# One-core two-block model: memory attention and index projection in one loop, the set-up in another order, pooled rows fetched apart

## What is computed

```python
# block 1
h = rmsnorm(x, g_mix);  proj = h @ w_in          # split into q_s k_s v_s | q_d k_d v_d | q_i k_i w_i | q_m | gates
o_swa = sliding_window_attention(rope(q_s), rope(k_s), v_s, sinks)      # 8 heads, window 128, blocks of 128
o_dsa = dsa_attention(rope(q_d), rope(k_d), v_d, rope(q_i), rope(k_i), w_i)   # 4 index heads, top 256 keys
o_mem = memory_cross_attention(q_m, mem_k, mem_v)                       # 4 heads, 256 memory rows
x = x + (sum of gate_b * (o_b @ w_proj_b)) @ w_out
x = x + square(relu(rmsnorm(x) @ w_mlp_in)) @ w_mlp_out                 # feed-forward 0
# block 2 (adaLN): mLSTM in two directions and a pooled branch y_b, then
x = x + gt1 * (concat(y_a, y_b) @ w_out_2)
x = x + gt2 * (square(relu(modulate(rmsnorm(x)) @ w_ff1)) @ w_ff2)      # feed-forward 1
```

## Time and profile before

| | us |
|---|---|
| three runs, median (lowest, highest) | 2640.07 (2639.22, 2640.80) |
| profiled execution | 2647.66 |
| its span | 2645.9 |
| PE busy in the span | 2482.5 (94%) |
| DVE, ACT, POOL busy | 1588.8, 1203.2, 834.6 |

### The profile page before, as it was taken

One profiled execution on the slowest core, in us unless ns is written; L12 is line 12 of the kernel. 1 busy time (PEld: TensorE's weight loads), 2 busy tenths in 40 slices (PEclk: granted clock), 3 DMA queues, 4 the chain that ended last, 5 costly groups with the idle time before them and its releaser, 6 DMA issues. The chain is left out here.

```text
span 2645.9 us, 32798 instructions
## 1 busy us (share of the span) xinstructions
PE 2482.5 (94%) x11852; PEld 2023.9 (76%) x11852; DVE 1588.8 (60%) x2820; ACT 1203.2 (45%) x2222; POOL 834.6 (32%) x748
## 2 busy tenths in 40 slices
PE   4997899999899999999999999999898999999997
PEld 3765688887677778887888887778776888878886
DVE  5347458988555687765545776334758444356666
ACT  6136346745511455554333453225526555443343
POOL 0222332221220066663252400005303565514242
PEclk9999899999999999999999999999999999999998
DMA  4102122323263256657754455424242444396354
GB/s 160 47 13 83 35 62 91 97 96 113 97 200 104 80 180 214 198 195 267 255 178 143 153 175 182 77 72 135 73 175 100 157 150 152 133 344 191 132 163 150
DMA packets 191187, 371.91 MB, mean 141 GB/s; under 512 B 13724, under 2 KB 58404, under 8 KB 190772
## 3 DMA queue, kind: packets, MB, share of 16 engines
q1 hardware_dynamic: 178676, 342.56, 39.2%
q10 hardware_dynamic: 8064, 14.68, 1.5%
q0 software_dynamic: 4288, 12.60, 1.5%
HBM read 269.05 MB, written 100.74 MB: 140 GB/s over the span
## 5 line engine op out<-in xcount | busy, mean ns | idle before, releaser
L2797 PE MATMUL bank<-hq_hi,wq_hi 128*128 128x512 f32 x896 | 352.7, 394 | 18.2 <-DVE hq_lo L1938 8.6
L2824 PE MATMUL bank<-ring_b_hi,ring_a_hi 128*128 128x512 f32 x896 | 350.7, 391 | 6.3 <-DVE hidden L1982 5.2
L2798 PE MATMUL bank<-hq_lo,wq_hi 128*128 128x512 f32 x896 | 350.6, 391 | 0.0
L2799 PE MATMUL bank<-hq_hi,wq_lo 128*128 128x512 f32 x896 | 350.5, 391 | 0.0
L2826 PE MATMUL bank<-ring_b_hi,ring_a_lo 128*128 128x512 f32 x896 | 350.1, 391 | 0.0
L2825 PE MATMUL bank<-ring_b_lo,ring_a_hi 128*128 128x512 f32 x896 | 350.1, 391 | 0.0
L2141 DVE TENSOR_TENSOR ring_a_lo<-a_raw,ring_a_hi 128x1024 fp32r<-128x1024 f32 x112 | 153.1, 1367 | 227.5 <-ACT ring_a_hi L1337 227.3
L1337 ACT ACTIVATE ring_a_hi<-a_raw 128x1024 fp32r<-128x1024 f32 x112 | 118.7, 1060 | 336.3 <-PE bank L2826 331.0
L1927 DVE TENSOR_TENSOR wq_lo<-unit_raw,wq_hi 128x512 fp32r<-128x512 f32 x160 | 164.4, 1030 | 108.9 <-ACT wq_hi L1185 106.0
L2797 PEld LDWEIGHTS bank<-hq_hi,wq_hi 128*128 128x128 f32 x896 | 169.4, 189 | 56.6 <-DVE hq_lo L1938 14.6
L2824 PEld LDWEIGHTS bank<-ring_b_hi,ring_a_hi 128*128 128x128 f32 x896 | 169.2, 189 | 42.7 <-DVE hidden L1982 6.1
(11 more groups left out here) (466 smaller groups left out, 5532.9 us busy)
## 6 DMA issues: line engine op xcount, KB each, us to landing
a_raw<-hidden_scratch SPq DMA_DIRECT2D x112, 512.0 KB, 3.3
hidden_scratch<-hidden SPq DMA_DIRECT2D x32, 1024.0 KB, 4.8
w_raw<-in_w_in SPq DMA_DIRECT2D x104, 256.0 KB, 2.8
hidden_scratch<-hidden SPq DMA_DIRECT2D x32, 768.0 KB, 3.6
unit_raw<-in_w_mlp_in SPq DMA_DIRECT2D x16, 1024.0 KB, 5.7
b_raw<-in_w_mlp_out SPq DMA_DIRECT2D x32, 512.0 KB, 4.4
unit_raw<-in_w_ff SPq DMA_DIRECT2D x16, 1024.0 KB, 5.4
b_raw<-in_w_ff SPq DMA_DIRECT2D x32, 512.0 KB, 4.7
```

Source lines behind the costliest of these rows:

```text
L2797: mm(o, lh[:, q, :], rh[:, q, :], start=(fresh and q == 0), stop=False, skip_group_check=True)
L2798: mm(o, lh[:, q, :], rl[:, q, :], start=False, stop=False, skip_group_check=True)
L2799: l = mm(o, ll[:, q, :], rh[:, q, :], start=False, stop=(q == 3), skip_group_check=True)
L2824: mm(o, ra_hi[r][:, e, js], rb_hi[r][:, e, :], start=(fresh and v == 0 and e == 0), stop=False, skip_group_check=True)
```

## The change

It has three parts.

1. **Memory attention and index projection in one loop.** The index weights are split inside the window attention: in each odd round u, ACT does `split_hi` of piece u // 2 behind `att_oh(u - 2)`, and DVE `split_lo` of it behind `att_norm(u - 1)`. Then one loop over v does, on PE, the scores of memory unit v + 1, half of index group v, the transposes of unit v, the other half of the group, the output of unit v - 1 and the rope transposes of group v - 1; ACT, DVE and POOL are ordered to match. The scores have one buffer (banks 0 and 1), the index group has bank 3, the attention output bank 2, the rope transposes XB[0] and XB[1]. POOL copies `k_mT` and `v_m` aside (`k_mem`, `v_mem`). The gate weights are split at the end of the loop.
2. **The set-up's other order.** `hq` 3 is made second on ACT instead of last, the weights of (2, 1) are split in `ff_setup`, `part_kept(k, 0, 2)` stands at the end of `ff_setup`, and PE makes (2, 1) between (6, 0) and (7, 0).
3. **Pooled rows.** The low parts of the second half are fetched ahead of the first load of `xs`, not behind the transposes; the high parts stay where they were.

```diff
-        MADE = SEQ[:3] + [(1, 1)] + [v for v in SEQ[3:] if v != (1, 1)]
+        MADE = SEQ[:3] + [(1, 1), (6, 0), (2, 1)] + [v for v in SEQ[4:] if v not in ((1, 1), (2, 1))]
...
-            return {1: (), 2: (), 5: (), 6: (), 7: (2, 5, 6, 7)}.get(p, (p,))
+            return {1: (), 2: (), 5: (), 6: (), 7: (5, 6, 7)}.get(p, (p,))
...
+                if not h:
+                    sp.dma_start(yT[1][1][:, 4:8, :].bitcast(f32), yl_d[:, HALF:S].rearrange("(k p) q -> p k q", p=P))\
+                        .then_inc(yb_in[1], 16)
                 if h:
                     sp.wait_ge(y_tr, 8)
-                    pooled_rows(1, [o[:, 4:8, :] for o in yT[1]])
+                    pooled_rows(1, [yT[1][0][:, 4:8, :]])
                 sp.dma_start(xs[:, 4 * h:4 * h + 4, :], x1_d[:, 4 * h:4 * h + 4, :]).then_inc(x2_in[h], 16)
...
                 if r == 16:
-                    for u in range(NSWA + 8):
+                    for u in range(NSWA - 2):
                         store(u)
+                    pool.wait_ge(qm_mm, 4)
+                    nc.gpsimd.tensor_copy(k_mem[:, :, :], k_mT[:, :, :]).then_inc(mem_kept.sem, 1)
+                    nc.gpsimd.tensor_copy(v_mem[:, :, :], v_m[:, :, :]).then_inc(mem_kept.sem, 1)
+                    for u in range(NSWA - 2, NSWA):
+                        store(u)
+                elif r >= 18:
+                    store(r - 2)
...
             def attend(u0, u1):
                 for u in range(u0, u1 + 2):
                         att_pt(u - 1)
                     if u0 <= u - 2:
                         att_oh(u - 2)
-                    if u1 == NSWA and u % 4 == 1 and u > 1:
+                    if u % 2 and u < u1:
+                        split_hi(C_IDX, 0, 20, [u // 2])
+                    if u % 4 == 1 and u > 1:
                         n = u // 4 - 1
                         act.wait_ge(qm_mm, n + 1)
                         A_(q_mT[:, 4 * (n // 2) + 2 * (n % 2):4 * (n // 2) + 2 * (n % 2) + 2, :],
                     split_hi(C_QM, 1, 12)
                 rope_evac(r, r // 8, r % 8)
             attend(0, NSWA)
-            split_hi(C_IDX, 0, 20)
-            attend(NSWA, NSWA + 8)
-            for r in range(16, 24):
-                rope_evac(r, 3, r % 8)
-                split_hi(C_GATE, 1, None, [r - 16])
+            att_exp(NSWA)
+            for v in range(10):
+                u = NSWA + v
+                if v >= 2:
+                    rope_evac(14 + v, 3, v - 2)
+                if v < 7:
+                    att_exp(u + 1)
+                if v < 8:
+                    att_pt(u)
+                if 1 <= v < 9:
+                    att_oh(u - 1)
+                if v >= 7:
+                    split_hi(C_GATE, 1, None, range(2 * v - 14, 2 * v - 12))
+            split_hi(C_GATE, 1, None, range(6, 8))
...
-                for p, i in ((5, 0), (6, 0), (7, 2), (4, 1), (3, 3)):
-                    if p == 6:
+                for p, i in ((5, 0), (3, 3), (6, 0), (7, 2), (4, 1)):
+                    if p == 3:
                         unit_hi(k, 1, 1)
+                    elif p == 7:
+                        unit_hi(k, 2, 1)
                     elif p == 4:
...
+                part_kept(k, 0, 2)
...
-                    elif p == 7:
+                    elif p == 7 and u:
                         part_kept(k, u, 2)
...
                         att_lo(u - 3)
                     if u0 <= u - 1 < u1:
                         att_norm(u - 1)
+                    if u % 2 and u < u1:
+                        split_lo(C_IDX, 0, [u // 2])
 
             for r in range(16):
                 if r == 0:
             link(nc.vector.memset(zero[:, :], 0.0))
             dve.wait_ge(r_tr, 16)
             attend(0, NSWA)
...
+            att_scores(NSWA)
+            for v in range(10):
+                u = NSWA + v
+                if v < 8:
+                    att_norm(u)
+                if v < 7:
+                    att_scores(u + 1)
+                if v >= 2:
+                    att_lo(u - 2)
+                    index_lo(v - 2)
+                if v == 0:
+                    for b in range(2):
+                        dve.wait_ge(at_od[b], 16 * NSWA)
+                if v < 8:
+                    rope_products(16 + v, 20 + v, 3, v)
+                else:
+                    split_lo(C_GATE, 1, range(3 * v - 24, 3 * v - 21))
+            split_lo(C_GATE, 1, (6,))
             for b in range(2):
                 dve.wait_ge(at_od[b], 16 * (NSWA + 8))
...
+            split_lo(C_GATE, 1, (7,))
...
-                low(6, 0, 10)
+                low(6, 0, 12)
                 difference(2, 3, 2, ht_p)
                 dve.wait_ge(xr_out.sem, xr_out.base + 128 * (k + 1))
                 hidden_added(k, 0, T_A11)
                 dve.wait_ge(ht_p.sem, ht_p.base + 4 * k + 2)
-                low(7, 2, 12)
+                unit_lo(k, 2, 1)
+                low(7, 2, 14)
                 difference(1, 1, 0, ht_p)
                 dve.wait_ge(ht_p.sem, ht_p.base + 4 * k + 4)
-                low(4, 1, 14)
-                low(3, 3, 16)
+                low(4, 1, 16)
+                low(3, 3, 10)
...
             def rope_transposes(r, kind, need):
                 pe.wait_ge(*need)
-                if r >= 2:
+                if kind == 3:
+                    pe.wait_ge(r_ev, r)
+                    pe.wait_ge(r_lo, r - 16)
+                elif r >= 2:
                     pe.wait_ge(r_ev, r - 1)
-                if r >= 18:
-                    pe.wait_ge(r_lo, r - 17)
-                x = XB[r % 2]
...
-                if kind == "swa" and u:
+                if u:
                     pe.wait_ge(at_s, u)
-                elif kind == "mem":
...
-                if u >= 2:
+                if u >= NSWA:
+                    pe.wait_ge(at_ol, u)
+                elif u >= 2:
                     pe.wait_ge(at_ol, u - 1)
...
+            def index_part(t, k0, k1):
+
+                g = 20 + t
+                if k0 == 0:
+                    pe.wait_ge(group_free, g)
+                for k in range(k0, k1):
+                    lh, ll = tok(hT, k, t)
+                    rh, rl = W[0][0][:, k, 0:452], W[0][1][:, k, 0:452]
+                    mm(bank[3][:, 0:452], lh, rh, start=(k == 0), stop=False)
+                    mm(bank[3][:, 0:452], lh, rl, start=False, stop=False)
+                    l = mm(bank[3][:, 0:452], ll, rh, start=False, stop=(k == 7))
+                if k1 == 8:
+                    l.then_inc(group_done, 1)
+
+            chunk_ready(C_IDX)
+            pe.wait_ge(mem_kept.sem, mem_kept.base + 2)
+            att_scores(NSWA)
+            for v in range(9):
+                u = NSWA + v
+                if v < 7:
+                    att_scores(u + 1)
+                if v < 8:
+                    index_part(v, 0, 4)
+                    att_transposes(u)
+                    index_part(v, 4, 8)
+                if v:
+                    att_out(u - 1)
+                    rope_transposes(15 + v, 3, (r_q, 16 + v))
             pe.wait_ge(at_ol, NSWA + 8)
 
             def gate_steps(n, k0, k1):
                 if k1 == 8:
                     l.then_inc(group_done, 1)
 
-            chunk_ready(C_IDX)
-            for r in range(16, 26):
-                if r < 24:
-                    natural(C_IDX, 0, 4 + r, r % 8, 452)
-                else:
-                    gate_steps(0, 2 * (r - 24), 2 * (r - 24) + 2)
-                if r >= 18:
-                    rope_transposes(r - 2, 3, (r_q, r - 1))
-
+            gate_steps(0, 0, 4)
```

## The result

The changed kernel takes 2654.91 us (median of 6 runs, 2652.6 to 2663.09) where the kernel before took 2640.99 (6 runs, 2639.22 to 2645.91): a ratio of 1.0053, 95% interval 1.0038 to 1.0068, 13.9 us slower (10.0 to 18.0). Forecast was 7.9 us slower, 2648.0.

The account below looks back on a forecast made before the run. PE was taken as the bound, with window attention a loop closing also over ACT and DVE. Loss 38.3 less gains 24.8, 2.4 and 3.2 made +7.9 us: 2655.6 profiled, 2648.0 as median; range 2625 to 2664.

Parts of the forecast that it names:

- What bounds the kernel: Whole kernel: PE busy 94% of the span; in window attention a loop over PE, ACT and DVE sets 4.68 us a unit.
- Part 1b, the detour: Window attention, odd rounds: from norm end N, DVE waits for ACT's split half; PE is 3.3 us later each round.
- Part 1b, the clock: Window attention, odd rounds: PE returns from its idle stretch at the lower clock, costing 2.0 us each, bounds 0 and 2.9.
- The end: End of window attention: round 15, with no scores behind it, pays 1.1 us, and 0.1 for the tail.
- Part 1a: Merged loop: PE-bound, 9.25 us a round, 83.0 us from first memory scores S to index scores; net gain 24.8 us.
- The gate weights: Index scores behind the merged loop: gate weights come late, so 2.5 us of the gain is counted back.
- Part 2: Both set-ups: (6, 1) starts 1.2 us earlier in each, gain 2.4 us; bounds gain 8, loss 1.
- Part 3: Pooled rows: the 1.6 us wait for low rows goes and the next wait shrinks; gain 3.2 us.
- From the profile to the median: Whole kernel: profiled execution lies 7.6 us above the median, so 2655.6 profiled becomes 2648.0 in terms of the median.
- Rival 1: Window attention: the clock holds through the pauses, an odd round costs 3.3 us only, sum -6.2, 2633.9 us; chance 0.20.
- Rival 2: Window attention: the split does not hold DVE up, only the gains remain, -30.4, 2609.7 us; chance 0.06.
- Rival 3: Merged loop is not PE's: three handovers a round, 2.5 us in each of 8 rounds, 2668 us; chance 0.14.

Follow-up runs that it names:

- e1: Changed kernel with both halves of the index split moved: ACT's ahead of the eviction of the transposes, DVE's between its scores and `att_lo`; 2622.22 us.
- e10: Changed kernel with 12 extra matmuls of 512 columns in PE's pause of each second window-attention round, six of seven pauses; 2648.44 us.
- e2: Changed kernel with only ACT's half of the index split moved ahead of the eviction, DVE's left behind the norm; 2627.35 us.
- e0: The kernel before, unchanged, run once more for a second profile; median of 10 runs 2642.82 us, profiled execution 2645.19 us.
- e5: The kernel before with only the set-up's other order added; ratio 1.0001 to the kernel before.
- e6: The kernel before with only the early fetch of the pooled rows' low parts added; ratio 0.9985 to the kernel before.
- e3: Changed kernel with PE's memory queries put ahead of the next scores in window attention; 2652.33 us.
- e4: Changed kernel with both halves of the index split moved and the set-up's order put back as before; 2621.77 us.

## Why the prediction was right or wrong

- **What bounds the kernel.** Right: window attention closes over DVE and ACT, and DVE had 0.75 us of room in a round, just enough for a piece (e1).
- **Part 1b, the detour.** Right in every step: `w_lo` at N+3.1 (forecast N+3.15), next norm N+7.57 (N+7.7), PE's wait 3.24 (3.4), loss 3.2 a round (3.3).
- **Part 1b, the clock.** It fell in all seven rounds, as taken; its size was 1.5 us, not 2.0 (e10). The end was under-priced: 37.0 - 7 x 4.7 = 4.1 us instead of 1.2. Some 1.4 of it lies in the seventh round's pair (15.50 us instead of 14.09, with the clock low from 251.5 to 258.3), and 2.8 behind the last window scores, where the detour comes on top of a wait that was there before (PE stands 4.05 us for 2.57) and the transposes behind it run at the lower level too. That the two misses nearly cancel, 37.0 against 38.3, is luck.
- **Part 1a.** The walk from S gave 83.0 and the trace gives 83.6, and its marks hold too: the second scores end at S+3.8 (forecast 3.7), the first transposes begin at S+6.7 (6.6), the second round's scores at S+10.2 (10.2). A round takes 9.39 us instead of 9.25. The gate weights cost 1.5 (50.2 - 48.7) instead of 2.5. Against the profile shown the gain is 26.7 - 1.5 = 25.1, forecast 24.8.
- **Part 2.** Wrong, sign included: +2.0 by the profiles instead of -2.4. (6, 1) did start 1.25 and 0.9 us earlier. The step that failed is to take that start for the gain: behind it 1.9 and 2.2 us are lost to the clock. I had myself forecast the wait of some 5 us before it and had the rows for what the clock does behind a wait, and let the sum end at the start of (6, 1), with the fall of the kernel before on one side of that mark and that of the new kernel on the other.
- **Part 3.** Right: 2.8 for 3.2; the wait of 1.6 is gone, that of 1.8 still stands at 0.9.
- **From the profile to the median.** Wrong by about 2 us. I took the 7.6 us by which the profiled execution lay above the median as spread over the whole. Some of it lay in the stage that the change replaces: 110.3 us there, 107.5, 106.6 and 106.7 in three other profiles with that stage unchanged. So the gain is 107.77 - 83.64 = 24.1 on the mean of these four, less 1.5, not 24.8. With the other means of the table the sum is 37.3 - 24.1 + 1.5 + 2.0 - 2.8 = +13.9 us, which is what the medians say; they are themselves known to 4 us only, so that it comes out to the tenth is luck. The forecast's +7.9 lacks 4.4 in part 2, 2.2 here and 0.4 in part 3, and has 1.0 too much in part 1b.
- **Why the two profiled executions differ by 5.2 us only.** The five parts, taken from those two profiles, add up to 37.0 - 26.7 + 1.5 + 1.9 - 2.8 = 10.9. Of the other 5.7 us, 4.6 lie in stretches that the change doesn't touch (3.0 from 1229 us to the pooled branch, 1.6 behind 2318 us in the kernel before): at 1236.4, 1533.4 and 2325.3 us the clock of the one before is low for 3.4 us each, and the changed kernel's isn't.
- **The rivals.** Rival 1 (the clock holds) is out by the clock rows, and e10 shows what it would have given. What the prediction said for it, that memory attention ran at the full clock with a pause of 1.48 in each unit, holds for the unit of the earlier trace rows only, which lies between two low stretches of the same stage (256.8 to 270.4 and 294.3 to 308.0 us):

```profile
256.80:270.40 13.60, 8.39 (x35) 0.50 0.26 79
270.40:294.30 23.90, 16.00 (x143) 1.00 0.15 45
294.30:308.00 13.70, 10.58 (x62) 0.50 0.13 39
```

  Rival 2 (no detour) is what e2 made of it, by an order of calls that the change doesn't have. Rival 3 (handovers in the merged loop) didn't come: behind the second scores, which it waits 1.56 us for, PE waits 0.19 us in the first round and 0.61 in the second, and from 297 to 360 us it is busy for 62.39 of 63.00 us.

## What to carry to other kernels

Before you slip a step into an in-order loop, write down for each engine what stands ahead of it and whom that waits for; a piece of work that two engines share in sequence must go in where the second engine's idle time lies, one stage later than the first's (here no cost against 4.7 us). Price a moved wait past the next mark at which both versions are in the same state, the clock's too, and not to the start of the instruction that was late. And before profile differences are turned into medians, take a second profile of the kernel before: here some 3 of the 7.6 us of its excess lay in the very stage that was to be replaced.

## What the runs showed of the hardware that I had not expected

- **The same wait, with the same instructions around it, can be followed by the lower level or not.** At the end of window attention the kernel before, e0, e5 and e6 have the same code, and PE waits 2.57 us in each. In before and e0 the clock was low for 3.4 us behind it (from 246.6 and 247.6 us), in e5 and e6 it stayed at the full level:

```profile
245.46 1.09 PE L2519 MATMUL bank<-ident,probs 128*128 128x128 f32 x8 [2.57 <-DVE probs L1639]
246.50:250.00 3.50, 3.50 (x17) 0.51 0.06 20
...
245.64 1.09 PE L2524 MATMUL bank<-ident,probs 128*128 128x128 f32 x8 [2.56 <-DVE probs L1643]
245.10:250.00 4.90, 3.21 (x24) 1.00 0.17 54
```

  Nor does a wait's length alone tell. The waits of 3.2 to 3.6 us in the changed kernel's seven rounds were each followed by the lower level, one of 3.05 us in e1, from 239.2 to 242.2, was not. In e3 two waits of 1.66 and 1.08 us were followed by it, in e2 one of 0.62 never. What decides is open.
- **Where the merged loop runs at the full level it repeats to the hundredth**: 83.64, 83.64, 83.65 and 83.64 us in after, e2, e1 and e4. In e3 and e10, where two low stretches fall into it, the same loop took 87.7 and 87.6. The stages before, with gaps in PE's work, took 106.6 to 110.3 us in four profiles of the same instructions. A loop that PE fills is also one that can be measured. The Trainium skill (TensorE: Matmul & The Clock Gate, the section on what is actually happening) says that how many matmuls run throttled at a kernel's start differs from run to run of the same kernel. The two profiles of the kernel before show such a difference over the whole kernel: 114.4 and 97.2 us at the lower level.
